# Down projection of a Strassen-style FFN: token sums stored by the up stage, weight sums on VectorE, no accumulating DMAs

## The reference, cut to what matters

```python
def _swiglu(x, w_in, w_out):
    gate, up = jnp.split(x @ w_in, 2, axis=-1)
    return (jax.nn.silu(gate) * up) @ w_out
...
    ff = _swiglu(_rms_norm(x, g[2]), ffn_in_w[layer], ffn_out_w[layer])
    x = x + _rms_norm(ff, g[3])
```

## Time and profile before

| | |
|---|---|
| median of three runs | 2502.28 us |
| profiled execution | 2508.05 us |
| its span, first to last instruction | 2506.0 us |
| mean granted TensorE clock | 0.964 of full speed |
| down stage of layer 0, first product to last | 845.0 to 1083.4 us |
| down stage of layer 1 | 2269.7 to 2495.7 us |
| TensorE busy | 2303.2 us (92%) |
| VectorE busy | 1442.2 us (58%) |

### The profile page before, as it was taken

One profiled execution on the slowest core, in us unless ns is written; L12 is line 12 of the kernel. 1 busy time (PEld: TensorE's weight loads), 2 busy tenths in 40 slices (PEclk: granted clock), 3 DMA queues, 4 the chain that ended last, 5 costly groups with the idle time before them and its releaser, 6 DMA issues.

```text
span 2506.0 us, 31448 instructions
## 1 busy us (share of the span) xinstructions
PE 2303.2 (92%) x10664; PEld 1901.2 (76%) x10664; DVE 1442.2 (58%) x2240; ACT 975.7 (39%) x1890; POOL 606.4 (24%) x676
## 2 busy tenths in 40 slices
PE   6999996999999999878888888978969999999997
PEld 5888784888888878666777777767758888888785
DVE  4333319665665677765555555563386655657776
ACT  3111116323222345633545545553352222323463
POOL 1000018322222023631111111110372222210236
PEclk9999996999999999989999999999979999999998
DMA  4111111223223579733232223222122232226787
GB/s 135 43 50 50 59 42 43 76 84 93 76 76 101 198 189 217 153 113 81 54 74 67 59 51 76 68 51 101 34 68 76 76 98 80 76 84 232 197 192 177
DMA packets 227567, 242.46 MB, mean 97 GB/s; under 512 B 16608, under 2 KB 155872, under 8 KB 225376
## 3 DMA queue, kind: packets, MB, share of 16 engines
q1 hardware_dynamic: 208640, 200.34, 27.4%
q0 software_dynamic: 15840, 28.84, 6.9%
q10 hardware_dynamic: 2944, 11.53, 1.2%
HBM read 184.05 MB, written 31.46 MB: 86 GB/s over the span
## 4 chain that ended last, share of the span: by engine, by line
PE 78%; DVE 7%; issue 5%; ACT 4%; POOL 3%; DMA 2%; SPq 1%; POOLq 0%; DVEq 0%; ACTq 0%
PE banks L935 33%; PE banks L986 12%; PE banks L786 11%; PE banks L1031 8%; PE banks L875 6%; PE banks L1081 2%; PE banks L1069 2%; PE banks L1094 2%; POOL raw_second L2440 1%; DMA hid_tile<-hid_spill 1%; PE banks L1108 1%; PE banks L825 1%; POOL rstd L2267 1%; POOL resid L2304 1%; DMA q_stack<-q_parts 1%
## 5 line engine op out<-in xcount | busy, mean ns | idle before, releaser
L935 PE MATMUL banks<-xb,up_split 128*128 128x512 f32 x3696 | 846.4, 391 | 11.1 <-DVE xb L1720 11.1
L935 PEld LDWEIGHTS banks<-xb,up_split 128*128 128x128 f32 x3696 | 698.6, 189 | 156.9 <-issue 11.6
L986 PE MATMUL banks<-down_split 128*128 128x512 f32 x1848 | 431.3, 394 | 18.9 <-DVE down_split L1891 15.8
L986 PEld LDWEIGHTS banks<-down_split 128*128 128x128 f32 x1848 | 349.6, 190 | 98.9 <-DVE down_split L1891 22.2
L1771 DVE TENSOR_TENSOR up_split<-sums,up_split 128x512 fp32r<-128x512 f32 x176 | 154.5, 879 | 163.5 <-ACT up_split L1273 163.3
L1031 PE MATMUL banks<-x_hi,w_second 128*128 128x512 f32 x768 | 227.9, 415 | 5.7 <-ACT v_t L1542 3.3
L2417 POOL TENSOR_TENSOR sums<-raw_up 128x512 f32<-128x512 f32 x88 | 115.3, 1312 | 395.4 <-DMA raw_up<-in_ffn_in_w 196.4
L786 PE MATMUL banks<-x_hi,w_first 128*128 128x512 f32 x768 | 184.4, 392 | 7.8 <-DVE x_lo L1683 7.8
L786 PEld LDWEIGHTS banks<-x_hi,w_first 128*128 128x128 f32 x768 | 145.0, 189 | 38.4 <-issue 5.7
L2478 POOL TENSOR_TENSOR resid<-o_parts 128x64 f32 (+1 forms) x128 | 47.4, 370 | 487.6 <-ACT o_parts L1586 487.6
L1031 PEld LDWEIGHTS banks<-x_hi,w_second 128*128 128x128 f32 x768 | 138.9, 196 | 28.3 <-issue 6.3
(11 more groups left out here) (177 smaller groups left out, 3430.5 us busy)
## 6 DMA issues: line engine op xcount, KB each, us to landing
raw_up<-in_ffn_in_w SPq DMA_DIRECT2D x88, 512.0 KB, 5.3
down_raw<-in_ffn_out_w SPq DMA_DIRECT2D x176, 256.0 KB, 4.8
hid_spill<-hid SPq DMA_DIRECT2D x88, 256.0 KB, 2.4
hid_tile<-hid_spill SPq DMA_DIRECT2D x66, 256.0 KB, 6.3
down_raw<-in_ffn_out_w POOLq DMA_DIRECT2D x66, 256.0 KB, 5.6
k_stack<-k_parts SPq DMA_DIRECT2D x32, 512.0 KB, 6.3
raw_first<-in_conv_in_w SPq DMA_DIRECT2D x24, 512.0 KB, 3.8
hid_tile<-hid_spill POOLq DMA_DIRECT2D x44, 256.0 KB, 6.8
```

Source lines behind the costliest of these rows:

```text
L935: mm = pe.matmul(bank(b_out), up_split[:, p, a, q * P:(q + 1) * P], xb[:, RIGHT_OF[p], b, q, :], start=(i == 0), stop=(i == len(passes) - 1))
L986: mm = pe.matmul(bank(b_out), side[:, a, 0, i * P:(i + 1) * P], side[:, b, 1, :], start=(p in (M3, M5, M1, M2) and first and j == 0), stop ...
```

## The change

- The up stage's DVE makes five token sums of each pair of hidden tiles (`mix`: M6, M5, M1, M7, M2), 128x512 each, in two buffers `hid_mix`; SP stores each in `hid_spill`, now one block for each product and pair. The plain halves that M3 and M4 need are stored as before, so seven blocks per pair are stored in place of four. A mix waits for the store of the mix two before it.
- The sums of the last pair stand behind `hidden_tokens(21)` and `split_low(down, 2)`, ahead of `block_sum` of q = 4 and `split_low` of q = 3.
- The down stage loads for each product one weight block and one token block into a ring of ten (`down_raw`), and for M1 with M4, M7 and M6 a second weight block into `down_second` (seven slots, three for the last ten). A second block waits for the sum that read its slot before; loads of the same product are behind it on SP.
- `block_sum` now makes weight sums only, in place in the slot: M3, M1, M4, M7, M6, again 55 per layer. ACT and DVE split both operands with one instruction of 128x1024 in place of two of 128x512.
- `add_blocks`, `turn_sign`, `hid_tile`, and the waits on the split of earlier products before the first attention chunk, are gone. The attention chunks are issued after the loads of q = 66.

```diff
...
-BLOCKS = 12
-BLOCKS_LAST = 8
-ADD_AHEAD = 5
-ADDS = 6
+DOWN_AT = (144, 148, 152, 156, 8, 12, 40, 44, 16, 20)
+SECOND_AT = (194, 212, 214, 160, 162, 164, 166)
+SECOND_LAST = 3
+MIXED = (M6, M5, M1, M7, M2)
...
+            if p in (M1, M4) and self.seconds and self.seconds[-1] == key:
+                self.second[q] = len(self.seconds) - 1
+                self.second_last[-1] = q
+                continue
+            self.second[q] = len(self.seconds)
+            self.seconds.append(key)
+            self.second_last.append(q)
+        self.second_slot = []
+        self.second_before = []
+        self.second_use = []
+        held = [None] * len(SECOND_AT)
+        self.second_uses = [0] * len(SECOND_AT)
+        many = len(self.seconds) - n + 1
+        for e in range(len(self.seconds)):
+            s = e % len(SECOND_AT) if e < many else (e - many) % SECOND_LAST
+            self.second_slot.append(s)
+            self.second_before.append(held[s])
+            held[s] = e
+            self.second_uses[s] += 1
...
-
-        return 0 if self.order[q][0] in (M2, M6) else 1
+        return 0 if self.order[q][0] in (M5, M2) else 1
...
-        hid_at = lambda f: ((8 + 2 * f if f < 8 else 68 + 2 * f) if f % 2 == 0 else
-                            (46 + 2 * f if f < 18 else 2 * f - 38))
-        hid_tile = [at(hid_at(f), f"hid_tile{f}", [SEQ]) for f in range(FT)]
...
-        hid_spill = nc.dram_tensor("hid_spill", (FT, P, SEQ), F32, kind="Internal").ap()
+        hid_spill = nc.dram_tensor("hid_spill", (7, FT // 2, P, HALF), F32, kind="Internal").ap()
...
+                if n % 2 == 0:
+                    sp.wait_ge(*hid2_done.at(ph, n + 1))
+                    sp.dma_start(hid_spill[M3, n // 2], hid[:, 0, 0:HALF]).then_inc(hid_out[0], 16)
+                else:
+                    sp.wait_ge(*hid1_done.at(ph, n + 1))
+                    sp.dma_start(hid_spill[M4, n // 2], hid[:, 1, HALF:]).then_inc(hid_out[1], 16)
+
+            def store_mixed(ph, n):
+
+                layer = 0 if ph == "up0" else 1
+                for p in MIXED[1:] if n % 2 else MIXED[:1]:
+                    g = mix_number(layer, p, n // 2)
+                    sp.wait_ge(*mix_made.at(ph, 5 * (n // 2) + MIXED.index(p) + 1))
+                    sp.dma_start(hid_spill[p, n // 2], hid_mix[g % 2][:]).then_inc(mix_out[g % 2], 16)
+
+            def load_second(layer, q):
+
+                e = plan.second[q]
+                s, ph = plan.second_slot[e], ("down0", "down1")[layer]
+                if plan.second_before[e] is not None:
+                    sp.wait_ge(*dve_sum.at(ph, plan.sums(plan.second_last[plan.second_before[e]])))
+                elif e == 0:
+                    sp.wait_ge(*up_done.at(("up0", "up1")[layer], PRODUCTS * FT))
+                elif e == 1:
+                    for b in range(2):
+                        sp.wait_ge(mix_out[b], 16 * len(range(b, 5 * plan.pairs * (layer + 1), 2)))
+                f, half = plan.seconds[e]
+                sp.dma_start(down_second[s][:], ffn_out_w[layer][f * P:(f + 1) * P, half * HALF:(half + 1) * HALF]) \
+                    .then_inc(second_in[s], 16)
+
+            def load_product(layer, q):
+
+                p, m = plan.product(q)
+                s, up, down = q % len(DOWN_AT), ("up0", "up1")[layer], ("down0", "down1")[layer]
+                if q >= len(DOWN_AT):
+                    sp.wait_ge(*down_lo.at(down, 2 * (q - len(DOWN_AT) + 1)))
+                elif q == 0:
                     sp.wait_ge(*up_lo.at(up, PRODUCTS * (FT - 2) + 6))
                     sp.wait_ge(*summed.at(up, 4 * (FT - 1)))
+                elif q == 2:
+                    sp.wait_ge(*up_lo.at(up, PRODUCTS * (FT - 1) + 6))
+                    sp.wait_ge(*summed.at(up, 4 * FT))
+                elif q == 4:
+                    sp.wait_ge(*up_done.at(up, PRODUCTS * (FT - 1) + 1))
+                elif q == 6:
+                    sp.wait_ge(*up_done.at(up, PRODUCTS * (FT - 1) + 6))
+                elif q == 8:
+                    sp.wait_ge(*up_done.at(up, PRODUCTS * FT))
+                if q in plan.second and plan.second[q] != plan.second.get(q - 1):
+                    load_second(layer, q)
+                if p in MIXED:
+                    g = mix_number(layer, p, m)
+                    sp.wait_ge(mix_out[g % 2], 16 * (g // 2 + 1))
                 else:
-                    sp.wait_ge(*up_lo.at(up, PRODUCTS * FT))
...
+                    b = 0 if p == M3 else 1
+                    sp.wait_ge(hid_out[b], 16 * (layer * plan.pairs + m + 1))
+                f, half = plan.weights(q)
+                sp.dma_start(weights(q), ffn_out_w[layer][f * P:(f + 1) * P, half * HALF:(half + 1) * HALF]) \
+                    .then_inc(down_in[s], 16)
+                sp.dma_start(tokens(q), hid_spill[p, m]).then_inc(down_in[s], 16)
 
             def load_ffn(layer):
-                up, down = ("up0", "down0") if layer == 0 else ("up1", "down1")
-                NP = plan.pairs
+                up = ("up0", "up1")[layer]
                 load_set(up, layer, 0)
                 load_set(up, layer, 1)
-                for n in range(FT):
+                for n in range(FT - 1):
                     if n + 2 < FT:
                         load_set(up, layer, n + 2)
-                    elif n == FT - 2:
...
                     else:
...
+                        load_product(layer, 0)
+                        load_product(layer, 1)
+                    if n:
+                        store_mixed(up, n - 1)
                     store_hidden(up, n)
-                for m in range(4, NP):
...
-                for c in range(5 * NP, plan.first_of_last):
-                    load_block(down, layer, c)
-                for c in range(plan.first_of_last, plan.blocks):
-                    load_block(down, layer, c)
-                    if layer == 0 and c == plan.first_of_last + 5:
-
-                        sp.wait_ge(*down_lo.at(down, 2 * plan.before_last))
+                store_mixed(up, FT - 2)
+                for q in range(2, len(DOWN_AT)):
+                    load_product(layer, q)
+                store_hidden(up, FT - 1)
+                store_mixed(up, FT - 1)
+                for q in range(len(DOWN_AT), QN):
+                    load_product(layer, q)
+                    if layer == 0 and q == 66:
                         load_projection(0, 0)
                         load_projection(1, 0)
...
-                if n == chunk0["attn"]:
-
-                    act.wait_ge(*down_lo.at("down0", 2 * plan.before_last))
...
-                    act.copy(high[:, 0, :], hid_half(2 * m, 1)).then_inc(down_hi.sem, 1)
+                down_landed(act, ph, q)
+                if plan.makes(q):
                     act.wait_ge(*dve_sum.at(ph, plan.sums(q)))
-                    act.copy(high[:, 1, :], both[:, 1, :]).then_inc(down_hi.sem, 1)
-                elif p == M5:
-                    block_in(act, ph, plan.block(q, 0))
...
+                dve.tensor_tensor(down_split[:, q % DOWN_RING, 1], down_raw[q % len(DOWN_AT)][:],
+                                  f32(down_split[:, q % DOWN_RING, 0]), ALU.subtract) \
+                   .then_inc(down_lo.sem, 2)
...
+                down_landed(dve, ph, q)
+                if p == M3:
+                    down_landed(dve, ph, q + 1)
+                    other = weights(q + 1)
...
+                    second_landed(dve, ph, q)
+                    other = second(q)
+                dve.tensor_tensor(weights(q), weights(q), other,
+                                  ALU.subtract if p in (M3, M4) else ALU.add).then_inc(dve_sum.sem, 1)
+
+            def mix(ph, p, m):
+
+                g = mix_number(0 if ph == "up0" else 1, p, m)
+                if g >= 2:
+                    dve.wait_ge(mix_out[g % 2], 16 * (g // 2))
+                for n in (2 * m, 2 * m + 1)[:1 if p == M6 else 2]:
+                    dve.wait_ge(*hid1_done.at(ph, n + 1))
+                    dve.wait_ge(*hid2_done.at(ph, n + 1))
+                a11, a21, a12, a22 = (hid[:, i, j * HALF:(j + 1) * HALF] for i in range(2) for j in range(2))
+                out_ = hid_mix[g % 2][:]
+                if p == M5:
+                    ins = dve.scalar_tensor_tensor(out=out_, in0=a11, scalar=-1.0, in1=a12,
+                                                   op0=ALU.mult, op1=ALU.subtract)
+                else:
+                    a, b, op = {M6: (a21, a11, ALU.subtract), M1: (a11, a22, ALU.add),
+                                M7: (a12, a22, ALU.subtract), M2: (a21, a22, ALU.add)}[p]
+                    ins = dve.tensor_tensor(out_, a, b, op)
+                ins.then_inc(mix_made.sem, 1)
 
...
+                    if n >= 2:
+                        dve.wait_ge(*mix_made.at(ph, 5 * (n // 2)))
...
+                    if n and n % 2 and p == 1:
+                        mix(ph, M6, n // 2)
+                    elif n and n % 2 == 0 and p in (1, 2, 5, 6):
```

(10 more changed lines are left out.)

268 lines of the change are left out of this document (44 added, 224 removed).

## The result

| | before | after |
|---|---|---|
| median of four runs each, same chip | 2502.27 us | 2483.36 us (2480.76 to 2486.42) |
| ratio, 95% interval | | 0.9918 (0.9900 to 0.9936) |
| span of the profiled execution | 2506.0 us | 2484.6 us |
| VectorE busy | 1442.2 us | 1490.4 us |

18.9 us less, where 8.0 were forecast (2494.3, range 2485 to 2506). The time lies just under the range, at the rival "the relief is whole" (2483.9), which had a chance of 0.15. The two profiled executions stand 5.8 and 3.1 us over their medians, so their spans differ by 21.4, not by 18.9.

The account below looks back on a forecast made before the run. TensorE, busy 92% of the span, was taken as the bound, so only its waits could be won. Terms -4.4 + 4.1 + 6.3 + 2.0 = 8.0 us off the median of 2502.28 gave 2494.3, range 2485 to 2506.

Parts of the forecast that it names:

- the relief is whole: Rival, chance 0.15: layer 0's tail +11.1, layer 1's +3.2, +4.1 in the middle, no turn loss; 18.4 off, 2483.9 us.
- The up stage, priced at nothing: Both up stages: VectorE's idle time hides 76 us of added token sums, so no gain or loss.
- The turn, -2.8: Up to down, both layers: TensorE waits 2.4 us before product 3 in place of 1.04, 1.4 worse per layer.
- late stores: Rival, chance 0.15: M5's and M1's stores land late at the turn; 2506.9 us with a landing of 7.7 us.
- The half of 1.6 for the slow stretch: After the turn's wait, half of a 1.6 us slow TensorE stretch charged per layer, -1.6 us together.
- After product 23, +4.1: Down stages: POOL's additions start 2 us earlier, waits 2.61 and 2.51 become 1.3: +2.5, and +1.6 for layer 1's slow stretch.
- Layer 0's tail, +6.3: Last products of layer 0's down stage: waits fall from 12.83 to 8.1 us, +2.3 for clock and turn, 0.7 lost.
- It has no lead when product 66 starts: Layer 0's tail: VectorE starts product 66 without lead, 0.80 us wait in front, and gets ten more weight sums.
- The rival with VectorE in the DMA's place: Rival, chance 0.20: ten VectorE sums on the path of layer 0's tail take 6.9 us of the gain; 2501.2 us.
- Layer 1's tail, +2.0: End of layer 1's down stage: wait 4.89 falls to 2.55, matmuls 10.70 to 10.02, +3.0; sums cost 0.7 and 0.3.
- Outside the down stages, 0: Everything but the two down stages, attention part included: no gain or loss forecast, 0 us.

Follow-up runs that it names:

- mix_twice: Changed kernel with each up-stage token sum of pairs 0 to 9 made twice, 100 more VectorE instructions; 2485.95 us, ratio 0.9929.
- c12_late: Changed kernel with GpSimd's four `sum_c12` additions held until ScalarE's four copies and VectorE's weight sum of product 25 are done; 2484.9 us, ratio 0.9922.
- dma_ahead: c12_late plus one plain 256 KB DMA that POOL issues directly in front of the four `sum_c12` additions; 2491.18 us, one execution.
- before_noadd: Kernel before with POOL's accumulating DMAs and the waits on them left out, so second blocks are missing; ratio 0.9917.
- before_plain: Kernel before with POOL's 110 accumulating DMAs as plain transfers, same queue places and waits; ratio 0.9943.
- after_pad: Changed kernel with 64 one-column VectorE memsets at the start of layer 0's up stage; 2484.91 us, one execution.
- before_pad: Kernel before with 64 one-column VectorE memsets at the start of layer 0's up stage; 2503.42 us, one execution.

## Why the prediction was wrong

**The up stage, priced at nothing: right.** mix_twice hides 123 us more.

**The turn, -2.8: right, by the forecast chain.** -3.2. The sums M7 and M2 waited 2.97 us for the stores (3.57 from issue to landing in the chain of waits, 2.1 forecast). The Trainium skill (DMA: Bandwidth & Descriptors, Queues, rings and completion order) has a store's increment behind every earlier write of its engine; the trace of layer 0 agrees in the order: the last load in front landed at 850.9, the plain half's store at 851.5, M5's at 852.1, M1's at 852.8, and once these were through, the next stores took 2.0 and 2.5 us. But the loads in front had been asked for 3 us earlier, so the stores were 1.5 us over the forecast and far from 7.7, and "late stores" did not come. The half of 1.6 for the slow stretch was a whole one in each layer.

**After product 23, +4.1: wrong in its reason, and in its size.** The forecast had VectorE kept out again, only earlier and between other instructions. c12_late shows that the time doesn't matter; dma_ahead shows that the DMA issue in front does. The changed kernel has none, so the lock-out goes whole: 5.1 us of waits where 2.5 were forecast. The 1.6 of layer 1's slow stretch did not come on top, because the wait in front of product 3 makes a slow stretch of its own (146.37 us of matmuls for 57.44 and 88.92 before). The Trainium skill (SBUF — State Buffer, Who interferes with whom) says that a VectorE instruction with two inputs in SBUF contends with a GpSimd instruction that reads SBUF, and calls the pair of ports that they share an exclusive lock. The 1.1 us that each VectorE instruction loses beside one POOL addition agree with it; the 5.3 us over four additions go beyond one instruction, and only behind a DMA issue.

**Layer 0's tail, +6.3: the step that failed.** It took VectorE's state at product 66 from the trace before: "It has no lead when product 66 starts". That lack of lead came from POOL's second transfers: before_noadd, without them, has no wait between products 56 and 67, while before_plain, which has them as plain DMAs, keeps one of 2.05 ahead of product 66. VectorE after, in that stretch, the splits (L1811) of products 66 to 69, the sums (L1827) of 68 to 70 between them, and the start of `add_m2`:

```profile
1027.91 1.21 DVE L1811 TENSOR_TENSOR down_split<-down_raw,down_split 128x1024 fp32r<-128x1024 f32 x1
1029.05 0.68 DVE L1827 TENSOR_TENSOR down_raw<-down_raw,down_second 128x512 f32<-128x512 f32 x1
1029.94 1.23 DVE L1811 TENSOR_TENSOR down_split<-down_raw,down_split 128x1024 fp32r<-128x1024 f32 x1 [0.21 <-ACT down_split L1353]
1031.08 2.39 DVE L1827 TENSOR_TENSOR down_raw<-down_raw,down_second 128x512 f32<-128x512 f32 x1
1033.39 1.21 DVE L1811 TENSOR_TENSOR down_split<-down_raw,down_split 128x1024 fp32r<-128x1024 f32 x1
1034.53 0.68 DVE L1827 TENSOR_TENSOR down_raw<-down_raw,down_second 128x512 f32<-128x512 f32 x1
1035.13 1.21 DVE L1811 TENSOR_TENSOR down_split<-down_raw,down_split 128x1024 fp32r<-128x1024 f32 x1
1036.27 0.68 DVE L1936 TENSOR_TENSOR acc_tile<-banks,acc_tile 128x512 f32<-128x512 f32 x1
```

Product 66 starts at 1029.6 (ten products of 2.75 us after 1002.08) and its split ends at 1029.1: half a microsecond of lead where the trace before has 0.80 of wait. From that start the split of 67 ends at S + 1.6, of 68 at S + 5.0, of 69 at S + 6.8 (forecast 1.9, 6.0, 7.9). The single costs were near, the sum beside `scale_chunk` among them (2.39, 1.7 more than alone, where 2 were put).

The whole miss lies ahead of the first turn: +2.9 where the terms give -2.0. Of these 4.9 us, 1.95 are the three small waits before products 64 to 66, which the forecast left standing; 0.7 is the sum of product 67, priced on the path and off it; 1.1 is the turn's own wait (1.16 for 0.6 and 1.7); and the same 156 matmuls took 35.74 us in place of 36.85. Behind the first turn +8.2 agrees with +8.3, but by two errors against each other: the waits came to 5.18 (0.85, 1.82, 2.51) where 5.8 were forecast, and the matmuls and turns gave back 1.6 where it had 2.3.

So layer 0 gave +11.1, the number of "whole relief"; that rival's own terms (12.83 less 3.5, and 2.3) add up to 11.6. That the whole time lies at its 2483.9 is partly luck: it had no loss at the turn, where 3.2 us went, and nothing from outside the down stages, where 4.5 came from. The rival with VectorE in the DMA's place had asked for 6.9 us of sums on the path; some 1.5 were.

**Layer 1's tail, +2.0: mis-sized at two places.** The same lead: three waits of .4 became one of 1.11, and no loss of 1.0 came; that is +3.0 in place of +1.3. And the clock: 10.70 fell to 8.47, not to 10.02. In all kernels the merged products took 10.49 to 11.27 us behind a wait of 4.4 to 5.3 us (5 of 5), but behind 2.5 to 2.6 us 8.45 to 8.50 in 19 cases and 9.88 to 10.09 in ten. The forecast took the one row it had, a slow one; after_pad, in layer 0, and the changed kernel differ in just this, at a granted clock of 1.00 and 0.50 behind the same wait of 2.51 us.

**Outside the down stages, 0: missed.** 3.7 us between them, of which some 2.3 go with the count of VectorE's instructions (after_pad, before_pad) and the rest is within what this part varies by; and 0.8 us that stay open: layer 0's down stage starts between 843.87 and 848.94 over all kernels of the study.

## What to carry to other kernels

A lag that an engine shows beside the thing you remove may be a part of it: leave the thing out in thought for the whole stretch before you take a state of the trace as the start of your own timeline. Work that must wait for a store belongs behind work that doesn't: four sums moved by one or two products were worth 8 us here, nearly half of what the whole change gave. A difference in a loop that nothing touched is to be shifted with a few idle instructions before it is called noise or gain.

## What the runs showed of the hardware

- Behind a DMA issued by GpSimd, its next four additions ran back to back (4.99 to 5.31 us) and kept VectorE out of all four; with a memset, or nothing, in front, the two engines took turns (6.90 to 7.99 us). It holds for plain and accumulating DMAs.
- As plain DMAs, in the same queue and with the same waits, the 110 accumulating ones made the kernel before 14 us faster (0.9943).
- 64 one-column VectorE instructions some 860 us earlier brought two stalls of 2.9 us or more into one kernel and took two of 2.75 out of another. In all 18 kernels the stalls go with more packets on the queue for instructions (72 to 78 against 64 to 68).
- Behind waits of 2.5 to 2.6 us the granted clock fell in some executions and not in others: the same 36 matmuls took 8.45 to 8.50 us 19 times and 9.88 to 10.09 ten times.
- A VectorE sum or split beside one GpSimd addition took 1.1 us more (0.68 to 1.78, 1.22 to 2.31).
